# Adaptive-modulation sums in the feed-forward loops: other places for the last tiles of VectorE and the last sum of TensorE

## The reference

```python
def swiglu(h, wg, wu, wd):
    return (jax.nn.silu(h @ wg) * (h @ wu)) @ wd
...
    for i in range(DEPTH):                         # first block, DEPTH = 2
        mod = c_act @ ada_w[i] + ada_b[i]          # (1, 9 * 1024)
        sh1, sc1, g1, sh2, sc2, g2, sh3, sc3, g3 = jnp.split(mod, N_MOD, axis=-1)
        h = modulate(rms_norm(x, ln_ffn1[i]), sh1, sc1)
        x = x + 0.5 * g1[:, None, :] * swiglu(h, ffn1_wg[i], ffn1_wu[i], ffn1_wd[i])
        ...                                        # attention or spatial gating, then ffn2, then a norm
...
def conv_ffn(h, w_up, conv_w, conv_b, w_down):     # second block
    a, v = jnp.split(h @ w_up, 2, axis=-1)
    a = depthwise causal convolution of width 3 over a, + conv_b
    return (jax.nn.silu(a) * v) @ w_down
```

## Time and profile before

| | |
|---|---|
| median of three runs | 1780.48 us |
| profiled execution: its own time | 1780.48 us |
| its span (first to last instruction) | 1778.9 us |
| PE busy | 1722.3 us, 97% |
| DVE busy | 1428.6 us, 80% |
| ACT busy | 912.1 us, 51% |
| POOL busy | 406.9 us, 23% |
| mean granted clock of TensorE | 0.993 |
| read from memory | 408.90 MB, 231 GB/s over the span |

### The profile page before, as it was taken

How to read it: one execution, slowest core, us unless ns; L and a number is a source line. 1 busy time by engine, 2 the same in 40 slices (tenths; PEclk the granted TensorE clock), 3 DMA queues, 4 the chain that set the end, 5 groups by cost and what they waited for, 6 DMA issues and landing times. The chain is left out here.

```text
span 1778.9 us, 36307 instructions
## 1 busy us (share of the span) xinstructions
PE 1722.3 (97%) x13995; PEld 1670.2 (94%) x13995; DVE 1428.6 (80%) x1842; ACT 912.1 (51%) x1274; POOL 406.9 (23%) x669
## 2 busy tenths in 40 slices
PE   6999999999999999999999999899999998899998
PEld 3999999999999999989999998889999997699998
DVE  4777898688779888877977899869988998678555
ACT  3433377764335433456533366566444666665444
POOL 4322311013223222120122344421322121301000
PEclk9999999999999999999999999999999998999999
DMA  9998857458986888756698856335988592147550
GB/s 334 370 335 272 300 188 257 154 172 310 326 280 237 286 291 299 258 188 215 233 332 268 303 182 231 108 119 188 322 300 290 144 247 95 48 132 259 167 188 24
DMA packets 261792, 411.44 MB, mean 231 GB/s; under 512 B 21950, under 2 KB 204414, under 8 KB 261560
## 3 DMA queue, kind: packets, MB, share of 16 engines
q1 hardware_dynamic: 223816, 288.57, 49.1%
q0 software_dynamic: 36720, 119.36, 19.1%
q10 hardware_dynamic: 1152, 2.10, 0.4%
HBM read 408.90 MB, written 2.63 MB: 231 GB/s over the span
## 5 line engine op out<-in xcount | busy, mean ns | idle before, releaser
L2749 DVE TENSOR_TENSOR lo<-raw,hi 128x2048 fp32r<-128x2048 f32 (+1 forms) x257 | 581.6, 2265 | 180.3 <-ACT hi L2572 179.9
L2572 ACT CAST hi<-raw 128x2048 fp32r<-128x2048 f32 (+1 forms) x266 | 498.7, 1877 | 387.9 <-PE dacc L2272 194.1
L2270 PE MATMUL up<-operand_hi,hi 128*128 128x256 f32 x1952 | 553.1, 283 | 2.3 <-DVE lo L2749 2.2
L2271 PE MATMUL up<-operand_lo,hi 128*128 128x256 f32 x1952 | 552.3, 283 | 0.0
L2272 PE MATMUL up<-operand_hi,lo 128*128 128x256 f32 x1952 | 552.3, 283 | 0.0
L2049 POOL DMA_DIRECT2D ada<-in_ada_w_dram x448 | 259.9, 597 | 815.5 <-DVE ada_acc L2785 750.3
L2270 PEld LDWEIGHTS up<-operand_hi,hi 128*128 128x128 f32 x1952 | 374.4, 192 | 3.7 <-DVE lo L2749 3.3
L2272 PEld LDWEIGHTS up<-operand_hi,lo 128*128 128x128 f32 x1952 | 374.5, 192 | 0.0
L2271 PEld LDWEIGHTS up<-operand_lo,hi 128*128 128x128 f32 x1952 | 374.5, 192 | 0.0
L2785 DVE SCALAR_TENSOR_TENSOR ada_acc<-ada,c_col,ada_acc 128x512 f32<-128x512 f32 x420 | 318.9, 759 | 13.8 <-DVE ada_acc L2785 0.9
L2270 PE MATMUL dacc<-act_hi,hi 128*128 128x256 f32 x1056 | 298.9, 283 | 2.6 <-DVE act_lo L2962 2.6
(11 more groups left out here) (453 smaller groups left out, 2692.1 us busy)
## 6 DMA issues: line engine op xcount, KB each, us to landing
ada<-in_ada_w_dram POOLq DMA_DIRECT2D x448, 256.0 KB, 4.6
raw<-in_ffn_wg_dram SPq DMA_DIRECT2D x88, 512.0 KB, 5.3
raw<-in_ffn_wu_dram SPq DMA_DIRECT2D x88, 512.0 KB, 5.1
raw<-in_ffn_wd_dram SPq DMA_DIRECT2D x88, 512.0 KB, 5.5
raw<-in_ffn_w_up_dram SPq DMA_DIRECT2D x88, 512.0 KB, 4.5
raw<-in_ffn_w_down_dram SPq DMA_DIRECT2D x46, 512.0 KB, 4.4
raw<-in_hg_w_in_dram SPq DMA_DIRECT2D x32, 512.0 KB, 6.0
raw<-in_attn_w_qkv_dram SPq DMA_DIRECT2D x24, 512.0 KB, 7.5
```

The lines of the kernel that those rows point to most:

```text
L2270: pe.matmul(o, stat[0], mov[0], start=start, stop=False, skip_group_check=True)
L2271: pe.matmul(o, stat[0], mov[1], start=False, stop=False, skip_group_check=True)
L2572: last = act.copy(put(slab(hi, s, SPL)), take(slab(raw, s, RAW)))
L2749: last = dve.tensor_tensor(put(slab(lo, s, SPL)), take(slab(raw, s, RAW)), put(slab(hi, s, SPL)).bitcast(F32), ALU.subtract)
```

## The change

Two things are written otherwise; no instruction is added or taken away.

```diff
@@ PE, ffn(p)
-                if v is not None and p not in five_vectors:
-                    ada_sum(v)
+                if v is not None:
+                    ada_sum(v + 4 if p in five_vectors else v)
                 down(FI - 1, stop=True)
-                if p in five_vectors:
-                    ada_sum(v + 4)
@@ DVE, ffn(p)
-                    iteration(3, it, v + 1 if more else None, 0, (0, 0, 4), summed=v if more else None)
+                    iteration(3, it, v + 1 if more else None, 0, (0, 0, 3), summed=v if more else None)
...
-                    iteration(4, it, v + 1 if more else None, 4, (2, 0, 2) if conv else (1, 1, 2))
+                    iteration(4, it, v + 1 if more else None, 3, (2, 3, 0))
```

## The result

The changed kernel takes 1795.39 us (median of four runs, 1792.34 to 1798.29), against 1781.08 us of the kernel before in the same comparison: ratio 1.0079, 95% interval 1.0065 to 1.0092. It is slower, as forecast (1788.5), but by 14.3 us in place of 8.0, and outside the range (1784.3 to 1792.0). The profiled execution has a time of 1798.73 us, a span of 1797.1 us and a mean clock of 0.984.

What follows compares the result with a forecast made beforehand. PE, busy 97% of the span, was taken as the bound; F0, F1, F3 +1.8, F2 +0.2, C0 +3.7, loads +0.6 and clock +1.7 gave +8.0 us on 1780.48: 1788.5 us, range 1784.3 to 1792.0.

Steps and rivals of the forecast that it cites:

- What bounds it: Whole kernel: PE is busy 97% of the span, with no wait left to remove in the loops.
- the number 0.58: F0's end: spare time in us ahead of down(10), 229.47 - 228.89, on which the change turns.
- The sum: Ahead of down(10): its 0.81 us on PE is free only where down(10) would wait anyway.
- C0: End of C0: six tile instructions, 4.53 us, delay down(10); the sum hides, net +3.7 us (3.0 to 5.3).
- the rival of a stalling loop: C0's loop begins to stall, with one microsecond left: 8.0 + 4.5, 1793 us; chance 0.10.
- The term of a tile's load: Last trip of each F phase: tile 7 lands late, 0.15 us each, 0.6 in all (0 to 2.0).
- The bound of 2.0: Upper bound in us of the term for late tile loads in the F phases, taken as 0.6.
- The clock term: Behind C0's gap, grown from 0.75 to about 4.5 us: clock drop costs 1.7 us (0 to 3.4).
- 6.3 forecast: All places without a clock drop: +6.3 us, 1786.8 us; as a rival, chance 0.22.
- The base: Starting time of the sum: 1780.48 us of the profiled execution, which is also the median.
- F2: End of F2: same shift, but G's wait of 1.34 us takes up the rest, +0.2 us (-0.8 to +0.6).

Runs made afterwards that it cites:

- e6: Changed kernel with four tiles at the end of iteration 3 and (1, 3, 0) in iteration 4: 1787.51 us, +4.5 us against the kernel before.
- e9: Kernel before with the tile placement of e6 and the sum ahead of down(10) in F0 to F3 only, C0 as before: 1782.15 us against 1783.55.
- e11: e6 with C0's gap filled by unused matmuls, 2 ahead of the sum and 9 behind: 1785.27 us, +1.7 us against the kernel before.
- e4: Kernel before with only the sum moved ahead of down(10), tiles as before: 1801.23 us, +18.8 us.
- e1: Kernel before with the change (tiles and sum) in F0 to F3 only, C0 as before: 1787.56 us against 1782.43, +5.1 us.
- e5: Changed kernel with unused matmuls filling the gaps ahead of down(10) in all five phases: 1792.75 us, +9.8 us against the kernel before.
- e8: Changed kernel with unused matmuls filling only C0's gap (8 and 10): 1790.18 us, +7.2 us against the kernel before.
- e10: The changed kernel run once more, nothing else altered: 1798.82 us against 1783.55 for the kernel before, +15.3 us.
- e7: Kernel before with 12 unused matmuls in G's gap of 3.3 us, where PE waits for DVE: 1784.79 us against 1782.98.

## Why the prediction was right in direction and wrong in size

- **What bounds it, and the number 0.58.** Right. PE had no wait to give back, and the spare time ahead of down(10) was used up. Where no load was late (F1, and all F phases of e6, e9 and e11) down(10) waited 0.59 to 0.60 us, as worked out.
- **The sum.** Right: it hides in the gap. Alone it costs 18.8 us (e4), since it waits for the last tile.
- **C0.** The start of down(10) was right: 4.6 us later in its position, 4.53 forecast. Its trips stayed at 35.4 us; the rival of a stalling loop is out.
- **The term of a tile's load was mis-sized: 0.6 us, against 1.9 (0.53 + 0 + 0.42 + 0.93 over the 0.60 us in F0 to F3).** The step that failed was not the landing but what was taken from it: the prediction's own rows gave 226.1 against 225.8, 0.3 us late, and it took 0.15 and nothing for what a longer gap brings. The second piece, put at 6.3 us, landed in 6.5 in F0 and in 6.9 in F3. In other executions the waits differ: F3's down(10) waited 1.08 to 2.15 us in e1, e5, e8 and e10, F0's 0.60 to 1.62. The bound of 2.0 in the text holds the waits in the profile, not the price with what follows from them: e1 and e9, with and without late loads, are 6.5 us apart by their medians and 2.7 in their traces.
- **The clock term was mis-sized: 1.7 us, against 5.** For C0 the 1.7 us were right: the filled gap costs 1.5 us less (e5 and e8 against the changed kernel), 2.2 less in e11 against e6. The step that failed was to look for a drop in C0 alone, where the gap was largest, and to judge gaps by PE's idle time: in F0 the sum and 1.13 us of idle time were followed by a window at 0.57, while gaps of 0.60 us behind the sum never were in e6, e9 and e11. In the changed kernel's two profiles one F phase each had a drop, F0 (1.5 us) and F3 (2.7). Over the 64 executions the time of the kernel before falls by 10 us for each 0.01 of mean clock, over the 26 of the changed one by 11. At 0.990 the fits give 1784.8 and 1792.4: 7.6 us are late starts and waits (6.3 forecast), and 12.5 - 7.6 = 4.9 us are clock. This split is an estimate, since 0.990 lies at the edge of both sets and the clock is recorded to 0.001; the traces agree roughly: 1.8 (F, e9) + 3.4 (C0, e5) + 1.9 (loads) = 7.1 us without the clock, and 3.1 and 4.3 us of clock at the five places in the changed kernel's two profiles.
- **The base.** The sum was made against 1780.48 us, a fast one of the executions of that kernel; the median of 64 is 1783.06. The 2.6 us between are more than a third of the miss of 6.9 us; loads (1.3) and clock (3.3) make up the rest. Its profile had a clock of 0.993, the mean is 0.9917.
- **F2.** The net +0.2 us was right where no load was late (0.1 to 0.2 in e6, e9 and e11); with the late load it was 0.6. But G's wait was to shrink to 0.9 us, and it stayed at 1.33, also in e6, e9 and e11 without a late load (1.34). It is a step of DVE behind PE's own last product and moves with it; it was no spare time.

By the Trainium skill (TensorE: Matmul & The Clock Gate, Part 1 on the HAM clock gate) activity is what holds the clock up. The filled gap of C0 at 1.00, against 0.51 unfilled, agrees.

What stays open: what decides whether the clock falls behind an F gap of 0.8 to 2.2 us (7 of 19 did), how often it falls at each place over many executions, and the differences of up to 5 us between the medians and the sums of the places (e8, e9, e10, e7). One profile of each kernel cannot show these.

## What to carry to other kernels

Work that is moved ahead of a wait on a saturated engine must fit into that wait's spare time, since what goes beyond it is paid (0.5 to 0.7 us at an F end here), and the loads of the moved work have to be counted again: moving their trigger by 2.1 us (issue against the end of down(9), the changed kernel against e6) made a load late here that was not late in the profile before. When a change opens a gap on TensorE, price the gap twice, once for its length and once for the matmuls behind it at half clock, and take the tiny matmuls in it as part of its length: the idle time alone, 1.1 us in F0, would not have warned. Take the base of a sum from many executions, not from the profiled one.

## What the runs showed of the hardware that I had not expected

- A gap on PE of about 2 us with 0.95 us of sums of two columns in it can be followed by a low clock: F0 in the changed kernel, 0.57 in the window behind, down(10) 7.32 us in place of 5.76.
- The same kernel on the same inputs spreads over 9 us (1779.07 to 1787.98), and its mean clock over the executions goes with it, 10 us for 0.01.
- The load of a tile that was issued 2.1 us later, in a stretch with a DMA share of 0.90 in place of 0.84, landed in 5.2 and 6.9 us (its two pieces) in place of 3.7 and 5.5 (F3).
- Filling a gap does not give back the whole of a drop: of 3.4 us of full speed lost behind G's gap, 1.1 came back in e7's profile, since PE then waited 1.71 us for DVE.
